# RMS norm of a two-layer token backbone: inverse roots moved from a scaling copy on ScalarE into the transposing product on TensorE

## What is computed

```
def rmsnorm(x, g):
    xf = x.astype(jnp.float32)
    y = xf * lax.rsqrt(jnp.mean(xf * xf, axis=-1, keepdims=True) + EPS)
    return y.astype(x.dtype) * g
...
h_lat = rmsnorm(x, norm_g[i]) * (1.0 + scale[:, None]) + shift[:, None]
h_ctx = rmsnorm(ctx, norm_g[i]) * (1.0 + scale_c) + shift_c
```

## Time and profile before

| What | us |
|---|---|
| Median of 3 executions (lowest, highest) | 4328.07 (4322.29, 4328.58) |
| The profiled execution's own time | 4328.89 |
| Its span, first to last instruction | 4327.1 |
| Norm of layer 0: first load issued, last low half done | 57.6, 134.5 |
| Norm of layer 1: first load issued, last low half done | 3354.2, 3435.8 |
| Granted TensorE clock over the span | 0.959 |

### The profile page before, as it was taken

One profiled execution on the slowest core, in us unless ns is written; L12 is line 12 of the kernel. 1 busy time (PEld: TensorE's weight loads), 2 busy tenths in 40 slices (PEclk: granted clock), 3 DMA queues, 4 the chain that ended last, 5 costly groups with the idle time before them and its releaser, 6 DMA issues. The chain is left out here.

```text
span 4327.1 us, 80392 instructions
## 1 busy us (share of the span) xinstructions
PE 4002.4 (92%) x30036; PEld 3363.3 (78%) x30036; DVE 2584.8 (60%) x3235; ACT 2129.2 (49%) x4198; POOL 2061.7 (48%) x1527
## 2 busy tenths in 40 slices
PE   7699999999999969999999999969999599978779
PEld 2378788778778759999999999967887488867667
DVE  3234544544445458888888888866664433239953
ACT  4245556655655635555555555541111511149922
POOL 2255565555556547777777777752111422100032
PEclk9899999999999979999999999989999599999889
DMA  6245555555555556777777777754443333265254
GB/s 256 88 128 157 151 153 157 156 151 158 151 156 156 155 184 204 209 213 215 214 216 211 211 210 213 215 199 157 182 172 131 98 112 118 108 241 200 87 151 136
DMA packets 777423, 733.23 MB, mean 169 GB/s; under 512 B 111904, under 2 KB 703264, under 8 KB 760416
## 3 DMA queue, kind: packets, MB, share of 16 engines
q1 hardware_dynamic: 684032, 681.48, 50.1%
q10 hardware_dynamic: 93056, 47.19, 3.6%
HBM read 483.12 MB, written 245.33 MB: 168 GB/s over the span
## 5 line engine op out<-in xcount | busy, mean ns | idle before, releaser
L627 PE MATMUL pj_bank<-h_hi,pj_whi 128*128 128x512 f32 (+1 forms) x1920 | 728.1, 379 | 14.5 <-POOL pj_first L613 14.5
L627 PE MATMUL pj_bank<-h_lo,pj_whi 128*128 128x512 f32 (+1 forms) x1920 | 708.9, 369 | 0.0
L1416 ACT ACTIVATE dc_R<-dc_psE 128x256 f16<-128x256 f32 x864 | 284.9, 381 | 522.7 <-PE dc_psE L1292 522.3
L994 DVE RECIPROCAL pj_acc<-pj_acc 128x2304 f32<-128x2304 f32 x16 | 232.8, 14553 | 373.4 <-ACT pj_acc L900 373.4
L627 PEld LDWEIGHTS pj_bank<-h_hi,pj_whi 128*128 128x128 f32 x1920 | 364.0, 190 | 82.0 <-POOL pj_first L613 15.0
L783 POOL TENSOR_TENSOR pj_BD<-pj_E,pj_gi 128x512 f32<-128x512 f32 x144 | 161.6, 1122 | 547.5 <-ACT pj_E L934 547.5
L627 PEld LDWEIGHTS pj_bank<-h_lo,pj_whi 128*128 128x128 f32 x1920 | 364.2, 190 | 66.3 <-issue 8.8
L931 ACT ACTIVATE pj_E<-pj_E,pj_gi 128x128 f32<-128x128 f32 x576 | 183.9, 392 | 452.3 <-DMA pj_gi<-scratch_gates 452.0
L1481 DVE TENSOR_TENSOR dc_Y<-dc_psY,dc_pick 128x256 f16<-128x256 f32 x864 | 322.8, 415 | 108.7 <-PE dc_psY L1277 108.5
L627 PE MATMUL pj_bank<-h_hi,pj_first 128*128 128x512 f32 (+1 forms) x960 | 354.3, 369 | 0.0
L627 PE MATMUL pj_bank<-h_hi,pj_wlo 128*128 128x512 f32 (+1 forms) x960 | 353.9, 369 | 0.0
(11 more groups left out here) (281 smaller groups left out, 10638.1 us busy)
## 6 DMA issues: line engine op xcount, KB each, us to landing
dc_dd<-scratch_decays SPq DMA_DIRECT2D x288, 256.0 KB, 5.2
dc_tm<-scratch_tm SPq DMA_DIRECT2D x288, 192.0 KB, 3.1
pj_E<-scratch_cgrow SPq DMA_DIRECT2D x288, 128.0 KB, 3.7
scratch_decays<-pj_E SPq DMA_DIRECT2D x144, 256.0 KB, 3.7
scratch_decays<-pj_BD SPq DMA_DIRECT2D x144, 256.0 KB, 3.7
dc_fm<-scratch_fm SPq DMA_DIRECT2D x288, 128.0 KB, 3.1
dc_egr<-scratch_egrow SPq DMA_DIRECT2D x288, 128.0 KB, 3.5
scratch_o<-dc_ob SPq DMA_DIRECT2D x288, 128.0 KB, 3.5
```

What stands on the lines that cost most here:

```text
L627: i = pe.matmul(self.bank[blk][:, 0:n], l[b][:, k, :], r[:, k, at:at + n], start=(m == 0), stop=(m == 3 * KT - 1))
L994: dve.reciprocal(acc[:, 0:TOK], acc[:, 0:TOK]).then_inc(s["recip"], 1)
L1416: act.activation(all_cols(R[q][p], l, True), split4(quart(bE[p]), l), ACT.Copy).then_inc(eR[p], 1)
```

## The change

The scaling copy and its two `xn` buffers of 128x1024 go. In its place VectorE multiplies the identity by `rs`, a 128x128 diagonal matrix `diag` (two buffers), right after the reciprocal, for which it waits. TensorE no longer transposes `xn` with the identity: it makes a real f32 product of the raw block of x with `diag`, which transposes the block and scales its rows at once. The load of a tile into a used buffer waits for the product (`s_tr`) and no longer for the scaling copy. The diagonal for tile i waits for the product of tile i-2.

```diff
--- before.py
+++ after.py
@@ -176,7 +176,7 @@
         if layer == 0:
             gate_weights(nc, ctx, T)
         xt += [sb(f"x{i}", [P, D]) for i in range(1, XB)]
-        xn = [sb(f"xn{i}", [P, D]) for i in range(2)]
+        diag = [sb(f"diag{i}", [P, P]) for i in range(2)]
         h = [sb(f"h{i}", [P, KT, P]) for i in range(HB)]
         junk = sb("junk", [P, D], F16)
         ss, rt, rs = ([sb(f"{x}{i}", [P, 1]) for i in range(2)] for x in ("ss", "rt", "rs"))
@@ -189,8 +189,8 @@
         load = [sem(n + f"load{i}") for i in range(XB)]
         load1, s_first, s_split = [sem(n + f"load1_{i}") for i in range(2)], sem(n + "first"), sem(n + "split")
         s_gate_w = sem(n + "gate_w")
-        s_ss, s_rt, s_rs, s_xn, s_tr, s_mul, s_h, s_hi, s_lo, s_rows, s_row, s_turn, s_m1 = (
-            sem(n + x) for x in ("ss", "rt", "rs", "xn", "tr", "mul", "h", "hi", "lo", "rows", "row", "turn", "m1"))
+        s_ss, s_rt, s_rs, s_diag, s_tr, s_mul, s_h, s_hi, s_lo, s_rows, s_row, s_turn, s_m1 = (
+            sem(n + x) for x in ("ss", "rt", "rs", "diag", "tr", "mul", "h", "hi", "lo", "rows", "row", "turn", "m1"))
         ctx_of = lambda i: 1 if i < CCH else 0
 
         place = lambda buf, i: buf[:, :, i * P:(i + 1) * P]
@@ -217,7 +217,7 @@
             def _(sp):
                 def body(i):
                     if i >= XB:
-                        sp.wait_ge(s_xn, i - XB + 1)
+                        sp.wait_ge(s_tr, i - XB + 1)
                     for p, rows in rows_of(i):
                         sp.dma_start(xt[i % XB][p, :], rows).then_inc(load[i % XB], 16)
                     if layer == 1 and i == 2 * XB:
@@ -243,24 +243,22 @@
                         act.wait_ge(s_rs, i - 1)
                     act.activation(rt[i % 2][:], ss[i % 2][:], ACT.Sqrt, bias=T["eps"][:], scale=1.0 / D).then_inc(s_rt, 1)
 
-                def scale(i):
-                    act.wait_ge(s_rs, i + 1)
-                    if i >= 2:
-                        act.wait_ge(s_tr, i - 1)
-                    act.activation(xn[i % 2][:], xt[i % XB][:], ACT.Copy, scale=rs[i % 2][:]).then_inc(s_xn, 1)
-
                 def high(i):
                     act.wait_ge(s_h, i + 1)
                     act.activation(place(hi, i), h[i % HB][:], ACT.Copy).then_inc(s_hi, 1)
-                turns((0, stats), (1, scale), (3, high))
+                turns((0, stats), (3, high))
 
             @block.vector
             def _(dve):
                 def invert(i):
                     dve.wait_ge(s_rt, i + 1)
                     if i >= 2:
-                        dve.wait_ge(s_xn, i - 1)
+                        dve.wait_ge(s_diag, i - 1)
                     dve.reciprocal(rs[i % 2][:], rt[i % 2][:]).then_inc(s_rs, 1)
+                    dve.wait_ge(s_rs, i + 1)
+                    if i >= 2:
+                        dve.wait_ge(s_tr, i - 1)
+                    dve.tensor_scalar(diag[i % 2][:], T["ident"][:], rs[i % 2][:], None, ALU.mult).then_inc(s_diag, 1)
 
                 def modulate(i):
                     dve.wait_ge(s_tr, i + 1)
@@ -307,11 +305,11 @@
             @block.tensor
             def _(pe):
                 def turn(i):
-                    pe.wait_ge(s_xn, i + 1)
+                    pe.wait_ge(s_diag, i + 1)
                     if i >= 2:
                         pe.wait_ge(s_mul, i - 1)
                     for k in range(KT):
-                        t = pe.transpose(tp[i % 2][:, k, :], xn[i % 2][:, k * P:(k + 1) * P], T["ident"][:])
+                        t = pe.matmul(tp[i % 2][:, k, :], xt[i % XB][:, k * P:(k + 1) * P], diag[i % 2][:], start=True, stop=True)
                     t.then_inc(s_tr, 1)
                     if i in ROWS1:
                         k = ROWS1[i]
```

## The result

The changed kernel takes 4361.87 us (median of 4 runs, 4355.45 to 4364.56) against 4328.32 for the kernel before beside it (4 runs, 4322.29 to 4334.12): ratio 1.0081, 95% interval [1.0068, 1.0093]. It is slower by 0.8%, 33.6 us, and 0.9 us from the forecast of 4361. The profiled execution took 4362.14 us, its span is 4360.3 us.

The account below looks back on a forecast made before the run. ScalarE's 3.35 us norm turn was taken as the bound, hiding 3.3 us of add plus low half. Layer 0 +19.9 and layer 1 +13 raised 4328.89 to 4362, or 4361 us against the median; range 4350 to 4378.

Parts of the forecast that it names:

- The exclusion: In the norms, VectorE's add and GpSimd's low half do not overlap; one of each needs 3.3 us a turn.
- the new period: Norm turn after the change: 4.6 us, 1.25 us longer than now, because the add waits for the low half.
- T + 4.62: End of the next tile's add, counted from T, the end of this tile's add in the norm.
- 4.6 us order: Norm turn order where each add comes after the low half has begun and waits for it; 4.6 us a turn.
- ScalarE's lost delay: ScalarE's queue now holds each rounding copy late, so GpSimd works beside the PSUM product; the change takes this away.
- low half: GpSimd's instruction in the norms, h minus its rounded part; 2.39 us undisturbed.
- backlog: GpSimd getting a tile behind in the norms; the diagonal then waits for a low half while GpSimd catches up.
- Just covered, at zero: Layer 1's loads with three x buffers: square of i+3 comes 8.4 us after diagonal i, within two 4.6 us periods.
- the two periods from a diagonal to the square three tiles on: Layer 1's time allowed for products and load: two turns of 4.6 us, against 8.4 us needed.
- covered: TensorE's dearer turns, 3.7 us in layer 1 and about 2.0 in layer 0, stay hidden; at 3.3 us, 3.7 would not.
- no contention for the diagonal: Rival: diagonal does not contend with GpSimd, so a lasting backlog gives 3.3 us a turn; 4340 us, chance 0.20.
- The faster rival: Exclusion does not bind in the norms; VectorE's own work sets 2.8 us a turn; 4311 us, chance 0.06.

Follow-up runs that it names:

- b_spare_diag: The kernel before, with VectorE also making a diagonal that nobody reads, ScalarE and TensorE unchanged: 4351.10 us, ratio 1.0068.
- a_diag_act: The changed kernel, with the diagonal made by ScalarE between square and rounding copy instead of by VectorE: 4344.22 us, ratio 1.0065.
- a_ring4: The changed kernel, with four x buffers in layer 1 instead of three: 4357.60 us, ratio 1.0078.
- b_product: The kernel before, with the transposes of xn made as real f32 products with the identity, no diagonal: 4332.59 us, ratio 1.0032.
- a_fold: The changed kernel, with VectorE's product and add replaced by eight two-operand TENSOR_SCALARs reading PSUM: 4316.54 us, ratio 0.9995.
- b_fold_ring4: The kernel before, with eight two-operand TENSOR_SCALARs from PSUM for product and add, and four x buffers in layer 1: 4309.90 us, ratio 0.9981.

## Why the prediction was right, and where its steps were off

- **The exclusion and the new period**: right. T + 4.62 was worked out from the add's end; 4.60 was measured in 13 of layer 0's 17 intervals. Adds were forecast at 2.9 us and took 3.04, ScalarE's wait at 2.3 and was 2.18. That the 4.6 us order comes back after the weight split was also seen.
- **The total**: 0.9 us from the forecast is luck in part. The two norms were to bring 33 us and brought about 29 (18.7 and 10.4); stages that the change does not touch gave the rest, within their scatter.
- **The cause within it**: off. The prediction named ScalarE's lost delay. b_spare_diag keeps ScalarE's copy and loses 28.5 us; a_diag_act drops it, keeps VectorE's list short, and its layer 0 loses 3. In layer 0 the loss needs the diagonal on VectorE and does not need the freed ScalarE. In layer 1 that is shown from one side only, by b_spare_diag (11.6 us), since a_diag_act is slow there by another way. That the diagonal stands behind a low half and so brings the 4.6 us order back after a backlog was in the prediction, but for the time after the weight split; one waits 2.19 us already at 74.49.
- **Layer 0**: +19.9 forecast, its norm ends 18.7 us later. The first low half came 0.5 earlier, not 1.4; from it to the end the norm grew by 19.2, not 21.3.
- **Layer 1**: +13 forecast, +10.4 measured, by other parts. Only 5 intervals came to 4.6 us, where 11 were to grow. "Just covered, at zero" for the loads was wrong: squares wait for loads 66.2 - 43.6 = 23 us more than before. The step at fault is the two periods from a diagonal to the square three tiles on. In a steady turn of 4.6 us it is 5.5 us (a_ring4 above), and products and load need 2.4 + 4.2 = 6.6 us at least. It cost nothing in the end, as a_ring4 shows, since late tiles also break the 4.6 us order; without them nearly all intervals grow.
- **TensorE**: 2.0 us a turn at the high clock, 2.05 measured against 1.09 before, 1.9 times. The Trainium skill (TensorE: Matmul & The Clock Gate, Terms) has the transpose mode four times faster; the trace does not agree. That layer 1 would run at the low clock with 3.7 us was wrong: the granted clock was 0.87 in the window above and 0.78 over the whole norm, and about half of the turns took 2.05, the others 2.7 to 3.8. And "covered" was too good: by itself the dearer product cost 14 us by the ratio and 16 by the medians (b_product), hidden here under a turn that is longer for another reason, and it is what bounds layer 0 once the exclusion is gone (a_fold).
- **The diagonal**: 0.25 us taken, 0.29 measured; 0.585 us on average in layer 0 and 0.95 in layer 1, with its waits.
- **ScalarE's busy time**: 41 us less forecast, 33 measured. Its instructions in the two norms take 92.9 us where they took 133.3, so the copies' share is gone as worked out; all other stages together take 7 us more, and why was not looked into.
- **The rivals**: no contention for the diagonal falls (2.18 us behind a low half), its order of 3.3 us appears when the diagonal is elsewhere. The faster rival asked that the exclusion not bind; a_fold takes it away, and its layer 0 is 1.3 us shorter than before, not the 8.5 that 17 intervals of 0.5 us would bring: TensorE was the next bound, and the eight instructions take 0.2 us more than product and add.

## What to carry to other kernels

Before moving work off the busiest engine, write out for one turn when each of two engines asks for what they share: here a few tenths of a microsecond decided between 3.35 and 4.60 us, and an added 0.29 us made the average turn 1.2 us longer (b_spare_diag), four times its length. Price an added instruction by where it puts the ones behind it. And if a stage hangs on such an order, take one of the users away from the shared resource rather than tune the order: reading PSUM instead of SBUF did it. Then look again for what is busy without a pause: here it was TensorE in one layer and VectorE in the other, not the engine that the change had freed.

## What the runs showed of the hardware

- A TENSOR_SCALAR over 128x128 f32 from SBUF takes 0.29 us alone and 2.18 or 2.29 us behind a low half of GpSimd: this short form too waits out the other's instruction. The same operation with two operands, from PSUM, does not: 18 low halves beside 144 of them took 2.35 us on average in layer 1 of b_fold_ring4, against 2.52 in the kernel before. The Trainium skill (SBUF — State Buffer, Who interferes with whom) says that a VectorE instruction with at most one SBUF input, outside the two-port modes, does not contend; the runs agree.
- An instruction's busy time includes its wait for the other engine's instruction: adds that need 1.23 us when free lasted 3.04. So VectorE's +49 us are about the 27.6 of diagonals and 23.6 of longer adds (80.7 after, 57.1 before, both layers), while its work grew by 36 x 0.29 = 10 us.

The groups of b_fold_ring4 in layer 1's norm:

```profile
L272 DVE TENSOR_SCALAR norm_h<-norm_tp,coef 128x128 f32<-128x128 f32 x144 | 47.4, 401 | 13.2 <-PE norm_tp L314 12.0 <-POOL h_lo L289 1.2
L289 POOL TENSOR_TENSOR h_lo<-norm_h,h_hi 128x1024 fp32r<-128x1024 f32 x18 | 42.2, 2351 | 72.2 <-ACT h_hi L254 72.2
```
